# A mixture-of-experts stage fed by one DMA queue: down weights in one load, gate and up read by column pairs, a new load order

## The reference, cut to what matters

```python
hg = jnp.einsum('nd,edf->nef', t, w_gate[sl])   # 2048 -> 512
hu = jnp.einsum('nd,edf->nef', t, w_up[sl])     # 2048 -> 512
hid = jax.nn.silu(hg) * hu * comb[:, sl, None]
out = out + jnp.einsum('nef,efd->nd', hid, w_down[sl])   # 512 -> 2048
```

## Time and profile before

| | |
|---|---|
| median of 3 runs | 1551.53 us |
| profiled execution, its own time | 1551.65 us |
| its span, first to last instruction | 1549.8 us |
| TensorE busy | 1521.5 us (98%) |
| VectorE, ScalarE, GpSimd busy | 514.0, 222.5, 55.7 us |
| read from HBM | 476.66 MB |
| granted TensorE clock, mean | 0.999 |
| mixer and routing, up to G0 | to 619.4 us |
| experts | 619.4 to about 1538 us |

### The profile page before, as it was taken

One profiled execution on the slowest core, in us unless ns is written; L12 is line 12 of the kernel. 1 busy time (PEld: TensorE's weight loads), 2 busy tenths in 40 slices (PEclk: granted clock), 3 DMA queues, 4 the chain that ended last, 5 costly groups with the idle time before them and its releaser, 6 DMA issues.

```text
span 1549.8 us, 23417 instructions
## 1 busy us (share of the span) xinstructions
PE 1521.5 (98%) x10075; PEld 978.1 (63%) x10075; DVE 514.0 (33%) x1113; ACT 222.5 (14%) x485; POOL 55.7 (4%) x58
## 2 busy tenths in 40 slices
PE   9999999999999999999999999999999999999997
PEld 6888777778876445656556556556556556556553
DVE  2566348743583104121321321321321321321323
ACT  3002313222312203000000000000000000000003
POOL 0000121003020000000000000000000000000000
PEclk9999999999999999999999999999999999999999
DMA  9743332141236046999999999999999999999996
GB/s 349 239 160 109 110 110 88 50 166 46 89 110 272 0 175 259 380 402 420 409 430 434 432 426 435 427 430 435 432 425 434 427 431 435 432 425 430 431 430 255
DMA packets 61084, 479.60 MB, mean 309 GB/s; under 512 B 10561, under 2 KB 19282, under 8 KB 41042
## 3 DMA queue, kind: packets, MB, share of 16 engines
q1 hardware_dynamic: 60736, 478.55, 75.0%
q10 hardware_dynamic: 290, 0.23, 0.1%
HBM read 476.66 MB, written 2.10 MB: 309 GB/s over the span
## 4 chain that ended last, share of the span: by engine, by line
PE 70%; DMA 23%; DVE 4%; ACT 1%; issue 1%; POOL 0%; SPq 0%; DVEq 0%; ACTq 0%; POOLq 0%
PE bank L1094 21%; DMA ring<-in_w_up_dram 21%; PE bank L758 20%; PE bank L909 7%; PE bank L1119 7%; PE bank L1174 4%; PE bank L1052 3%; DMA ring<-in_w_down_dram 2%; DVE region_m L1729 1%; PE bank L847 1%; PE bank L827 1%; PE bank L674 1%; PE bank L850 0%; PE bank L856 0%; PE bank L1112 0%
## 5 line engine op out<-in xcount | busy, mean ns | idle before, releaser
L1094 PE MATMUL bank<-ring,region_m 128*64 128x256 f32 x4096 | 455.7, 381 | 7.0 <-DMA ring<-in_w_up_dram 7.0
L1094 PEld LDWEIGHTS bank<-ring,region_m 128*64 128x64 f32 x4096 | 290.6, 137 | 162.6 <-issue 12.6
L758 PE MATMUL bank<-region_u,ring 128*128 128x272 f32 (+2 forms) x1536 | 369.6, 393 | 0.0
L758 PEld LDWEIGHTS bank<-region_u,ring 128*128 128x128 f32 x1536 | 283.8, 190 | 52.3 <-issue 0.9
L1119 PE MATMUL bank<-region_qy,region_s 128*64 128x512 f32 x992 | 218.4, 592 | 0.5 <-issue 0.5
L1119 PEld LDWEIGHTS bank<-region_qy,region_s 128*64 128x64 f32 x992 | 71.8, 137 | 127.8 <-issue 119.1
L1964 DVE TENSOR_TENSOR region_s<-region_s,bank 128x256 f32<-128x256 f32 x32 | 13.5, 421 | 334.5 <-PE bank L1094 334.5
L1052 PEld LDWEIGHTS bank<-region_m,region_u 128*128 128x128 f32 x960 | 108.3, 192 | 11.7 <-issue 11.7
L1174 PE MATMUL bank<-region_m 128*128 128x512 f32 x256 | 114.1, 599 | 0.0
L1052 PE MATMUL bank<-region_m,region_u 128*128 128x128 f32 x960 | 111.2, 277 | 0.0
L1729 DVE SCALAR_TENSOR_TENSOR region_m<-region_qy,cols,region_m 128x256 f32<-128x256 f32 x240 | 106.7, 508 | 1.7 <-DVE region_qy L1757 0.5
(11 more groups left out here) (273 smaller groups left out, 823.0 us busy)
## 6 DMA issues: line engine op xcount, KB each, us to landing
ring<-in_w_gate_dram SPq DMA_DIRECT2D x31, 4096.0 KB, 32.7
region_qy<-in_w_down_dram SPq DMA_DIRECT2D x62, 2048.0 KB, 19.9
ring<-in_w_up_dram SPq DMA_DIRECT2D x28, 4096.0 KB, 21.8
ring<-in_w_in_dram SPq DMA_DIRECT2D x40, 1024.0 KB, 7.3
ring<-in_w_up_dram SPq DMA_DIRECT2D x8, 2048.0 KB, 10.5
ring<-in_w_out_dram SPq DMA_DIRECT2D x12, 1024.0 KB, 5.3
ring<-in_w_in_dram SPq DMA_DIRECT2D x16, 512.0 KB, 5.0
region_qy<-in_w_out_dram SPq DMA_DIRECT2D x4, 1024.0 KB, 13.0
```

Of the source, the lines that this page charges most:

```text
L758: last = mm(banks[n % 2][:, 0:width], slot[s][:, 512 * k + P * j:512 * k + P * (j + 1)], uT[:, 4 * g + k, T - width:T], start=g == k == 0, ...
L1094: last = mm(banks[is_up][CAP * i:CAP * (i + 1), 0:FE // 2], uTe[:, k, CAP * x_:CAP * (x_ + 1)], w[:, c0:c0 + FE // 2], start=k == 0, stop= ...
```

## The change

Four things are changed. (1) The down weights of an expert come in one load of 4 MB, with 4 rows (32 KB) for each partition, and D waits for the whole. (2) To match this order of rows, the gate and up products read, for `i` = 0, columns 0 and 1 of every four, and for `i` = 1 columns 2 and 3. (3) In the loop each gate load stands ahead of the up load, and the loads ahead of the loop are reordered. (4) At the end, D31 takes all parts of the first quarter before those of the second, and each of its two banks is evacuated by VectorE and ScalarE together. Down of expert 30 and 31 is still loaded in pieces.

```diff
-        down_v = w_down[0].rearrange("e (g p k) n -> e g p (k n)", p=P, g=2)
+        down_v = w_down[0].rearrange("e (p g k) n -> e g p (k n)", p=P, g=2)
+        down_all = w_down[0].rearrange("e (p k) n -> e p (k n)", p=P)
...
             def load_d(e, ahead, u):
-                if isinstance(u, int) and u + ahead == 0:
-                    sp.wait_ge(out_done, 4 * TT)
-                else:
+                sp.wait_ge(out_done, 4 * TT)
+                if not isinstance(u, int) or u + ahead > 0:
                     sp.wait_ge(down_done, u + ahead)
-                for i in (1, 0):
-                    sp.dma_start(down_w[i], expert_of(down_v, e, ahead, i)).then_inc(d_full[ahead][i], 16)
+                sp.dma_start(region_qy[:, 0:2 * BIG], expert_of(down_all, e, ahead)).then_inc(d_full[ahead], 16)
...
             def stream(e, u):
+                load_gate(e, 2, u, 0)
                 load_up(e, 1, u)
                 load_d(e, 0, u)
-                load_gate(e, 2, u, 0)
+                load_gate(e, 3, u, 1)
                 load_up(e, 2, u)
                 load_d(e, 1, u)
-                load_gate(e, 3, u, 1)
             def last_pair_of(u):
                 load_up(NE - 2, 1, u)
-                load_d(NE - 2, 0, u)
+                sp.wait_ge(down_done, u)
+                for i, full in ((1, d_full[0]), (0, last_even_full)):
+                    sp.dma_start(down_w[i], down_v[NE - 2, i]).then_inc(full, 16)
                 load_last_d(u)
...
             load_up_in_halves(1)
             load_gate(0, 3, 0, 1)
+            load_d(0, 1, 0)
             load_up_in_halves(2)
-            load_d(0, 1, 0)
+            load_gate(2, 2, 2, 0)
             load_up_in_halves(3)
             load_d(2, 0, 2)
-            load_gate(2, 2, 2, 0)
+            load_gate(2, 3, 2, 1)
             load_up_in_halves(4)
             load_d(2, 1, 2)
-            load_gate(2, 3, 2, 1)
...
-                            c0 = FE * k + FE // 2 * i
+                            quads = w[:, FE * k:FE * (k + 1)].rearrange("p (q i j) -> p i q j", i=2, j=2)
                             last = mm(banks[is_up][CAP * i:CAP * (i + 1), 0:FE // 2], uTe[:, k, CAP * x_:CAP * (x_ + 1)],
-                                      w[:, c0:c0 + FE // 2], start=k == 0, stop=k == KD - 1)
+                                      quads[:, i], start=k == 0, stop=k == KD - 1)
...
-                pe.wait_ge(d_full[x_][1], 16 * (p + 1))
+                pe.wait_ge(d_full[x_], 16 * (p + 1))
...
             def last_down(p, r):
...
-                pe.wait_ge(d_full[1][0], 16 * (p + 1))
+                pe.wait_ge(last_quarter_full[0], 16 * (r + 1))
                 for q in range(2):
-                    for n_f, f in ((2, 0), (3, 1)):
-                        if q == 0 and f == 1:
-                            pe.wait_ge(last_quarter_full, 16 * (r + 1))
-                        last = down_part(last_down_w, 1, n_f, f, q, LAST_DOWN_BANKS)
-                    last.then_inc((down_half, down_done)[q], 1)
+                    down_part(last_down_w, 1, 2, 0, q, LAST_DOWN_BANKS)
+                pe.wait_ge(last_quarter_full[1], 16 * (r + 1))
+                for q in range(2):
+                    down_part(last_down_w, 1, 3, 1, q, LAST_DOWN_BANKS).then_inc((down_half, down_done)[q], 1)
...
+            def last_take_y(u):
+                for q, done, ready in ((0, down_half, y_act), (1, down_done, last_y_act)):
+                    act.wait_ge(done, u + 1)
+                    c0 = 1024 + BANK * q
+                    act_fn(ypair[CAP:P, c0:c0 + BANK], banks[LAST_DOWN_BANKS[q]][CAP:P, :], ACT.Copy).then_inc(ready, 1)
...
+            def last_take_y(u):
+                for q, done, ready in ((0, down_half, y_dve), (1, down_done, last_y_dve)):
+                    dve.wait_ge(done, u + 1)
+                    dve.tensor_copy(ypair[CAP:P, BANK * q:BANK * (q + 1)], banks[LAST_DOWN_BANKS[q]][0:CAP, :]).then_inc(ready, 1)
```

More of the change, by code:

```diff
@@ L369, in hybrid_kernel @@
         up_full = sem("up_full")
-        d_full = [[sem(f"d_full{x_}{i}") for i in range(2)] for x_ in range(2)]
+        last_even_full = sem("last_even_full")
+        d_full = [sem(f"d_full{x_}") for x_ in range(2)]
         first_quarter = sem("first_quarter")
@@ L441, in hybrid_kernel @@
         down_half = sem("down_half")
-        last_quarter_full = sem("last_quarter_full")
+        last_y_dve = sem("last_y_dve")
+        last_y_act = sem("last_y_act")
+        last_quarter_full = [sem(f"last_quarter_full{i}") for i in range(2)]
         y_act = sem("y_act")
@@ L592, in load_d @@
             def load_d(e, ahead, u):
-                if isinstance(u, int) and u + ahead == 0:
-                    sp.wait_ge(out_done, 4 * TT)
-                else:
+                sp.wait_ge(out_done, 4 * TT)
+                if not isinstance(u, int) or u + ahead > 0:
                     sp.wait_ge(down_done, u + ahead)
-                for i in (1, 0):
-                    sp.dma_start(down_w[i], expert_of(down_v, e, ahead, i)).then_inc(d_full[ahead][i], 16)
+                sp.dma_start(region_qy[:, 0:2 * BIG], expert_of(down_all, e, ahead)).then_inc(d_full[ahead], 16)
             def load_last_d(u):
                 sp.wait_ge(gate_done, u + 1)
-                sp.dma_start(gate_w[0][:, BIG:], down_v[NE - 1, 1]).then_inc(d_full[1][1], 16)
-                for f, full in enumerate((d_full[1][0], last_quarter_full)):
+                sp.dma_start(gate_w[0][:, BIG:], down_v[NE - 1, 1]).then_inc(d_full[1], 16)
+                for f, full in enumerate(last_quarter_full):
                     part = slice(2048 * f, 2048 * (f + 1))
@@ L1121, in down_part, with down @@
                 return last
-            def down(p, x_, turned_between=None):
+            def down(p, x_, turned_between=None, r=None):
                 u = 2 * p + x_
@@ L1153, in last_down, with last_scatter @@
                         down_part(last_down_w, 1, n_f, f, q, LAST_DOWN_BANKS)
-                pe.wait_ge(d_full[1][0], 16 * (p + 1))
+                pe.wait_ge(last_quarter_full[0], 16 * (r + 1))
                 for q in range(2):
-                    for n_f, f in ((2, 0), (3, 1)):
-                        if q == 0 and f == 1:
-                            pe.wait_ge(last_quarter_full, 16 * (r + 1))
-                        last = down_part(last_down_w, 1, n_f, f, q, LAST_DOWN_BANKS)
-                    last.then_inc((down_half, down_done)[q], 1)
+                    down_part(last_down_w, 1, 2, 0, q, LAST_DOWN_BANKS)
+                pe.wait_ge(last_quarter_full[1], 16 * (r + 1))
+                for q in range(2):
+                    down_part(last_down_w, 1, 3, 1, q, LAST_DOWN_BANKS).then_inc((down_half, down_done)[q], 1)
+            def last_scatter(p, r):
+                pe.wait_ge(selw_ready, p + 1)
+                pe.wait_ge(y_dve, 2 * p + 2)
+                for i in range(8):
+                    if i == 1:
+                        pe.wait_ge(y_act, 2 * p + 2)
+                    if i == 2:
+                        pe.wait_ge(last_y_dve, r + 1)
+                    if i == 3:
+                        pe.wait_ge(last_y_act, r + 1)
+                    if i >= len(LAST_SCATTER_BANKS):
+                        pe.wait_ge(scatter_read, 8 * p + i - len(LAST_SCATTER_BANKS) + 1)
+                    mm(banks[LAST_SCATTER_BANKS[i % len(LAST_SCATTER_BANKS)]], sel_wT[:, P * (i // 4):P * (i // 4 + 1)],
+                       ypair[:, column(i)], start=True, stop=True).then_inc(scatter_done, 1)
             def scatter(p, sb=SCATTER_BANKS):
@@ L1199, in pair @@
                 if not first_pair:
-                    down(p, 0, 2 * p + 1 if last_pair else None)
+                    down(p, 0, 2 * p + 1 if last_pair else None, r)
                 if last_pair:
@@ L1217, in one_round @@
                 pair(r * PAIRS + PAIRS - 1, False, True, r)
-                scatter(r * PAIRS + PAIRS - 1, LAST_SCATTER_BANKS)
+                last_scatter(r * PAIRS + PAIRS - 1, r)
             one_round(0)
@@ L1478, in take_y @@
                     c0 = 1024 * v + BANK
-                    last = act_fn(ypair[CAP * x_:CAP * (x_ + 1), c0:c0 + BANK], banks[bank][CAP * v:CAP * (v + 1), :], ACT.Copy)
+                    last = act_fn(ypair[CAP * x_:CAP * (x_ + 1), c0:c0 + BANK], banks[DOWN_BANKS[1]][CAP * v:CAP * (v + 1), :], ACT.Copy)
                 last.then_inc(y_act, 1)
+            def last_take_y(u):
[3 more added lines that the diff above has]
+                    act_fn(ypair[CAP:P, c0:c0 + BANK], banks[LAST_DOWN_BANKS[q]][CAP:P, :], ACT.Copy).then_inc(ready, 1)
             def pair(p, last_pair):
@@ L1488, in pair @@
                     take_y(2 * p, 0)
[L1489 removed]
+                    last_take_y(2 * p + 1)
                 else:
@@ L1970, in take_y @@
                     c0 = 1024 * v
-                    last = dve.tensor_copy(ypair[CAP * x_:CAP * (x_ + 1), c0:c0 + BANK], banks[bank][CAP * v:CAP * (v + 1), :])
```

(10 more changed lines are left out.)

8 lines of the change are left out of this document (4 added, 4 removed).

## The result

The changed kernel takes 1567.79 us (median of 4 runs, 1566.52 to 1568.46) against 1551.28 us for the kernel before on the same chip (4 runs): ratio 1.0099, 95% interval 1.0086 to 1.0112. It is slower by 1%, and the prediction of 1552.5 us, with a range from 1549.0 to 1557.0, is wrong. The profiled execution has a span of 1566.7 us against 1549.8.

What follows compares the result with a forecast made beforehand. The load queue, at 29.21 us an expert against TensorE's 28.70, was taken as the bound. U2's 0.9 us wait and waits at D9 to D29 replace 7.9 us of waits: +1.0 us, so 1552.5 us, range 1549.0 to 1557.0.

Steps and rivals of the forecast that it cites:

- Column pairs: Gate and up products reading two of every four columns: taken to cost nothing.
- rival (b): Gate and up products: column pairs cost TensorE time; 1568 us at the weight load's 5%; chance 0.10.
- s: Extra time for each of the 64 gate and up blocks of 7.06 us; 0.35 us at 5%.
- the two clocks: Per expert in the new order: TensorE's own work at 28.70 us, the load queue at 29.13 us.
- One load for down: Down loads merged: saves 0.08 us an expert, queue at 29.13 us; D gives up 3.5 us of slack.
- Gate in front, and the end: Load order: early queue gaps close, but D waits from D9; down 29 lands at 1490.4, D31 ends at 1534.05.
- rival (c): Early gate loads: the queue runs dry, 1.5 us lost each restart, two make 1555.5 us; chance 0.17.
- The new end: D31's parts reordered: worth up to 0.9 us if its last load came last; expected hidden, so nothing.
- The evacuation by two engines: Copies of D31's banks at the end: nobody waited for them before, so nothing won.
- The floor of TensorE: End of D31 without waits for loads: 1525.7 us, from 1533.07 less 7.0 and 0.34.
- (a): Load queue: TensorE no longer waits for it, 6.5 us less, 1545.0 us; chance 0.13.
- The chances: Odds for the whole change: forecast 0.60; faster 0.13, the same 0.63, slower 0.24.

## Why the prediction was wrong, by its own steps

**Column pairs: the step that failed.** The working had both halves of the answer: "the weight load of the hidden turn reads with step 2 and takes 202 ns against 192", 5% more, and the sum for it in rival (b): s = 0.35 and 1568 us. It then took nothing, "since the nearest row is within a few per cent and a product is longer than its weight load". The measured s is 0.37 (5.2%), and pairs alone give 1567.0 us. The reason given was no reason: a product that reads 256 columns paid the same share as the weight load of 128, and 64 blocks pay it, 64 x 0.37 = 23.7 us of TensorE's time. With only 0.43 us an expert between the two clocks, a few per cent of 14 us was more than the gap. The prediction had even worked out that 1.7% decides, and named products that last longer as a sign that it was wrong: their mean is 390 ns, where it was 381. ScalarE's row at step 16, 1.84 times, had its counterpart too: a product with one column in each 16 bytes takes 14.63 / 7.06 = 2.07 times.

The Trainium skill (SBUF — State Buffer, in the section on the DMA port swizzle) has reads at full bandwidth from two hits in each 16-byte line. Here two hits cost 5.2% on a product's moving side (7.43 us against 7.06), against that rule, and one hit doubles the time; the measurement decides.

**One load for down.** The halves and the whole: right in kind. Without pairs the period of down landings is (1492.03 - 821.66) / 23 = 29.15 us, where 29.13 was forecast from a saving of 0.08. The Trainium skill (DMA: Bandwidth & Descriptors, section Measured) has 6.15 us for 1 MB and 79.0 us for 16 MB; its table is for loads issued from GpSimd, where these are issued by SyncE. The estimate of a fixed price from it (1.3 us by those two numbers, where the prediction wrote 1.2) is not seen in a full queue: a load less in each expert saves 0.06 us. That D gives up 3.5 us of slack costs nothing that the run with this edit alone can tell.

**Gate in front, and the end.** Right in mechanism, a little off in size: without pairs D31's end is 1.3 us later than forecast. Down 29 lands 1.6 us late. Of this 1.2 is there by down 6: 0.7 from the gate load that met an almost empty queue (rival (c), at half its price for one restart), and 0.5 that stays open. The other 0.4 comes from the period. That the closed gaps win nothing, since down 29 becomes the last load that is waited for, is what the profile of the kernel without pairs shows; that it is the order that does this, by putting off what is needed first, is shown, for one down load, by changing the order back at expert 14 (3.8 us).

**The new end.** "Worth up to 0.9 if it were last": 0.5 in the profile of the kernel with this edit alone, where the last quarter then comes just in time. The evacuation by two engines: nothing, as forecast.

**The floor of TensorE.** The 1525.7 us for the end of D31 without waits was too high. The list of waits counts only idle time, but an up block behind a wait also takes 7.15 us instead of 7.06, in the chain of before. From D3 on, 26 experts at 28.70 and the 43.6 us of the end give 734.71 + 746.2 + 43.6 = 1524.5. That is 1.2 us less, and it enters rivals (a) and (b), not the forecast.

**The chances.** Rival (b) had 0.10, at a price of 1568 us, which is what came. That it fits to a microsecond is partly luck: its floor was 1.2 us too high and its s of 0.35 gave 1.3 us too little. It had the only row of the trace that measured the new read, so it should have been the forecast, or at least lain inside the range.

## What to carry to other kernels

Where a price has only one row near it, use that row's price, not nothing; multiply it by how often it is paid and hold it against the gap between the two resources that are nearly equal. A layout that gives the loads longer runs is paid for by whoever reads it: four 4-byte columns in a row are free for a product, two cost 5%, one costs double. And of load orders: once the queue is the slower one, load first what is needed first; that was worth 3.8 us here. What it is worth to fill the queue's gaps before that, these runs could not tell from nothing.

## What the runs showed that I had not expected

Reads by every fourth column of a float32 moving operand double the product (14.63 against 7.06 us a block), while 64-column runs in a nested pattern are free (379 ns a record both). A down load merged from two 2 MB halves saves about 0.06 us (29.21 - 29.15) in a queue that is already full. And putting VectorE's register reads behind its last copy delays the first of eight additions by 1.1 us and the end by nothing that shows. Last, the same loads in the same order made U2 wait 0.7 us and 3.1 us, and the experts started at 619.5 or 621.2 us, from one execution to the next: more than several of the differences looked for here.
